# A two-layer decoder step with experts: the first chunk of layer 1's memory projection is computed inside pack 0 of layer 0's experts, and filling products take its place in layer 0's routing

## The reference, cut to what matters

```
for i in range(DEPTH):                       # both layers, before the trunk
    kv = rmsnorm(mem_prompt, mem_norm[i]) @ w_mem_kv[i]      # 256 x 1024 @ 1024 x 2048
    ...                                      # keys, values of layer i, also outputs
...
h = rmsnorm(x, norm_mix[i]);  z = h @ w_in
x = x + concatenate([mix, cross_attn(q, mem_k[i], mem_v[i])]) @ w_out
x = x + hier_moe(rmsnorm(x, norm_ffn[i]), ...)
```

## Time and profile before

| | us |
|---|---|
| median of the 3 timed executions | 1237.73 |
| lowest and highest | 1232.91, 1238.44 |
| the profiled execution | 1237.39 |
| its span, first to last instruction | 1235.6 |
| TensorE busy | 1170.5 (95%) |
| TensorE weight loads | 689.7 |
| VectorE busy | 356.5 |
| ScalarE busy | 154.2 |
| read from and written to HBM | 339.34 MB and 24.32 MB |

### The profile page before, as it was taken

How to read it: one execution, slowest core, us unless ns; L and a number is a source line. 1 busy time by engine, 2 the same in 40 slices (tenths; PEclk the granted TensorE clock), 3 DMA queues, 4 the chain that set the end, 5 groups by cost and what they waited for, 6 DMA issues and landing times.

```text
span 1235.6 us, 13751 instructions
## 1 busy us (share of the span) xinstructions
PE 1170.5 (95%) x5928; PEld 689.7 (56%) x5928; DVE 356.5 (29%) x870; ACT 154.2 (12%) x363; POOL 11.8 (1%) x22
## 2 busy tenths in 40 slices
PE   6999999999999998989999999999999999997886
PEld 5567776677554342436655656566667753432333
DVE  4222224112213141335224242424301022432225
ACT  2000002012111110110201011010200021110002
POOL 0000000000000000000000000000000000000000
PEclk9999999999999999999999999999999999999898
DMA  9953336833599999999234657392985469999994
GB/s 384 427 186 136 136 136 282 340 136 136 234 426 424 428 429 427 429 426 427 109 136 191 243 190 294 137 356 115 414 363 186 155 245 428 412 428 427 427 428 169
DMA packets 28159, 364.59 MB, mean 295 GB/s; under 512 B 3280, under 2 KB 3296, under 8 KB 5056
## 3 DMA queue, kind: packets, MB, share of 16 engines
q1 hardware_dynamic: 25200, 339.87, 67.2%
q10 hardware_dynamic: 1712, 19.17, 3.7%
q0 software_dynamic: 1184, 4.63, 1.0%
HBM read 339.34 MB, written 24.32 MB: 294 GB/s over the span
## 4 chain that ended last, share of the span: by engine, by line
PE 85%; DMA 12%; DVE 2%; issue 1%; ACT 1%; SPq 0%; DVEq 0%
PE bank L766 23%; PE bank L496 13%; DMA ring<-in_gu 11%; PE bank L604 7%; PE bank L582 5%; PE bank L401 5%; PE bank L849 5%; PE bank L406 4%; PE bank L636 4%; PE bank L614 3%; PE bank L820 1%; PE bank L452 1%; PE bank L930 1%; PE bank L419 1%; PE bank L475 1%; PE bank L911 1%
## 5 line engine op out<-in xcount | busy, mean ns | idle before, releaser
L766 PE MATMUL bank<-hT,ring 128*128 128x288 f32 x1088 | 268.2, 407 | 0.9 <-issue 0.9
L766 PEld LDWEIGHTS bank<-hT,ring 128*128 128x128 f32 x1088 | 205.7, 190 | 66.9 <-issue 12.0
L496 PE MATMUL bank<-arena,ring 128*128 128x288 f32 x640 | 158.5, 407 | 1.8 <-DVEq L1305 1.8
L496 PEld LDWEIGHTS bank<-arena,ring 128*128 128x128 f32 x640 | 120.2, 190 | 34.2 <-issue 2.2
L604 PE MATMUL bank<-ring,arena 128*32 128x512 f32 x944 | 115.3, 629 | 24.2 <-DMA ring<-in_gu 24.2
L582 PE MATMUL bank<-arena 128*128 128x512 f32 (+1 forms) x192 | 96.5, 628 | 0.2 <-DVE arena L1380 0.2
L604 PEld LDWEIGHTS bank<-ring,arena 128*32 128x32 f32 x944 | 30.4, 113 | 101.2 <-issue 82.5
L636 PE MATMUL bank<-arena 128*128 128x288 f32 x256 | 68.8, 413 | 2.8 <-issue 2.4
L401 PE MATMUL bank<-arena,ring 128*128 128x256 f32 x256 | 60.1, 398 | 9.4 <-DMA ring<-in_wkv 9.4
L582 PEld LDWEIGHTS bank<-arena 128*128 128x128 f32 (+1 forms) x192 | 31.5, 189 | 65.0 <-issue 63.9
L1397 DVE TENSOR_TENSOR xT<-xT,bank 128x288 f32<-128x288 f32 x128 | 58.2, 455 | 33.0 <-PE bank L636 29.2
(11 more groups left out here) (245 smaller groups left out, 846.4 us busy)
## 6 DMA issues: line engine op xcount, KB each, us to landing
ring<-in_gu SPq DMA_DIRECT2D x59, 2048.0 KB, 22.0
ring<-in_dn SPq DMA_DIRECT2D x32, 2048.0 KB, 19.8
ring<-in_rin SPq DMA_DIRECT2D x14, 2048.0 KB, 13.2
ring<-in_cin SPq DMA_DIRECT2D x8, 2048.0 KB, 24.5
ring<-in_kc SPq DMA_DIRECT2D x8, 2048.0 KB, 7.7
ring<-in_vc SPq DMA_DIRECT2D x8, 2048.0 KB, 10.5
ring<-in_st SPq DMA_DIRECT2D x8, 2048.0 KB, 10.4
out_rs<-ring ACTq DMA_DIRECT2D x8, 2048.0 KB, 8.4
```

The costliest lines, as they stand in the source:

```text
L496: mm = pe.matmul(bank[1 + o % 4][:, 0:T], w[:, k, :], cat[:, k, :], start=(k == 0), stop=(k == kt - 1))
L766: mm = pe.matmul(outs[o], w[:, o, k, :], src[:, k, :], start=(k == 0), stop=(k == KD - 1))
```

## The change

`MEMORY_IN` gets an entry for pack 0 (chunk 0), and chunk 0's weights leave the end of `SEQ_A`. So `pack_sequence(0)` puts them behind the four gate/up transfers of pack 0 and ahead of its down transfers: gate/up have now the places 24 to 27, chunk 0 the place 28, the down transfers 29 and 30 as before. Every later transfer keeps its place. `route(0)` has the filling products of `route(1)`. The two products of chunk 0 stand in pack 0 behind `pick(1)`, use PSUM banks 4 and 7 as those of the other chunks do (3 and 4 before), and are followed by the wait on ScalarE's copies. `memory_ahead(0)` is called from ScalarE's `experts` and no longer between its routing and the experts.

```
-SEQ_A = (... + [("vc0", c) for c in range(4)] + [("cout", c) for c in range(4)] + [("kv1", 0)])
-MEMORY_IN = {1: 1, 3: 2, 5: 3}
+SEQ_A = (... + [("vc0", c) for c in range(4)] + [("cout", c) for c in range(4)])
+MEMORY_IN = {0: 0, 1: 1, 3: 2, 5: 3}
...
-            KV_BANKS = ((0, 1, 2, 3, 4, 5, 6, 7), (3, 4, 4, 7, 4, 7, 4, 7))
+            KV_BANKS = ((0, 1, 2, 3, 4, 5, 6, 7), (4, 7, 4, 7, 4, 7, 4, 7))
...
             def route(i):
-                if i == 0:
-                    memory_kv(1, 0)
-                else:
-                    for _ in range(FILL):
-                        pe.matmul(bank[3][:, :], C("ident"), C("decay")[:, 0:512], start=True, stop=True)
+                for _ in range(FILL):
+                    pe.matmul(bank[3][:, :], C("ident"), C("decay")[:, 0:512], start=True, stop=True)
                 pe.wait_ge(S("htok_out"), KD * (i + 1))
                 pe.wait_ge(S("chosen"), i + 1)
...
-                if i == 0:
-                    memory_kv(1, 1)
-                else:
-                    pe.matmul(bank[3][:, :], C("ident"), C("decay")[:, 0:512], start=True, stop=True)
+                pe.matmul(bank[3][:, :], C("ident"), C("decay")[:, 0:512], start=True, stop=True)
...
-                    if L == 0 and i == 0:
-                        pe.wait_ge(S("kv1_out"), 2)
                     if L == 0 and i in MEMORY_IN:
                         j = 2 * MEMORY_IN[i]
                         memory_kv(1, j)
-                        pe.wait_ge(S("gt_out"), i)
+                        if i:
+                            pe.wait_ge(S("gt_out"), i)
                         memory_kv(1, j + 1)
                         pe.wait_ge(S("kv1_out"), j + 2)
...
             route(0)
-            memory_ahead(0)
             experts(0)
```

More of the change, by code:

```diff
@@ L55 @@
 SEQ_A = ([("kv0", c) for c in range(4)] + [("cin", c) for c in range(8)] + [("kc0", c) for c in range(4)]
-         + [("vc0", c) for c in range(4)] + [("cout", c) for c in range(4)] + [("kv1", 0)])
-MEMORY_IN = {1: 1, 3: 2, 5: 3}
+         + [("vc0", c) for c in range(4)] + [("cout", c) for c in range(4)])
+MEMORY_IN = {0: 0, 1: 1, 3: 2, 5: 3}
 def pack_sequence(l):
@@ L1032, in memory_ahead @@
                     dst = KT[:, 2 * j:2 * j + 2, :] if c < 2 else v3(V[:, j % 2, (c - 2) * 512:(c - 1) * 512], 2)
-                    act.activation(dst, v3(bank[(3, 4, 4, 7, 4, 7, 4, 7)[j]][:, :], 2), ACT.Copy) \
+                    act.activation(dst, v3(bank[(4, 7, 4, 7, 4, 7, 4, 7)[j]][:, :], 2), ACT.Copy) \
                        .then_inc(S("kv1_out"), 1)
```

## The result

Measured with 22 executions of each kernel, the changed one takes 1239.58 us (1237.24 to 1243.56) and the one before 1236.86 (1232.91 to 1239.12): a ratio of 1.0026, 95% interval 1.0018 to 1.0033. That is 2.2 to 4.1 us slower. The forecast was 3.0 us slower, 1240.7. It took 0.5% as the least that a measurement can tell; with 22 executions of each the interval is 0.15% wide, and 3 us are clear of no change. The profiled execution has a span of 1238.7 against 1235.6.

The account below looks back on a forecast made before the run. Layer 0's expert-weight transfers were taken as the bound. TensorE 10.8 us earlier, then 14.70 added: 3.9 late, less 0.9 in hand, gives 3.0 on the 1235.6 span; timed forecast 1240.7 us, range 1235.5 to 1244.0.

Parts of the forecast that it names:

- What bounds the stage: Layer 0's experts: weight transfers at 421 and 427 GB/s; landings set by the stretch's start and whether the queue runs dry.
- Part 1: Layer 0's routing: two products of 15.2 us removed, 14.50 us remain, first gate/up product 10.8 us earlier.
- Part 2: Chunk 0 in pack 0: 14.70 us added on TensorE, unhidden, so pack 1's gate/up products come 3.9 us later.
- Part 3: Ring order of transfers: costs nothing; pack 1's first gate/up issue at 319.4, 1.7 us earlier.
- The sum: Pack 2's down transfers: queue dry for 3.8 us, second landing 3.0 us late, kept to the end; 1240.7 us.
- dry a second time at 386.9: Pack 2's second down transfer, forecast issue 386.8, finds the queue empty again and lands 7.7 us later.
- the 0.9 us that the second down transfer had in hand: Pack 2: its landing took 8.6 us, 0.9 more than on an empty queue, so 3.9 late becomes 3.0.
- The earlier start: Rival: queue doesn't run dry at 377, all landings keep the 1.7 us, 1236.0; chance 0.10.
- The clock: Rival: two more 3.4 us half-clock stretches between 303 and 387 make landings 6.4 us late, 1244.1; chance 0.06.

Follow-up runs that it names:

- The ring order alone: Kernel before with only chunk 0's weights moved behind pack 0's gate/up weights, its products still in layer 0's routing: 1247.33 us, 1.0080.
- the filler run: Kernel before with five filling products of 512 columns added in pack 0 behind the wait for ScalarE's copies: 1238.32 us, 1.0015.
- the chunks apart: Changed kernel with the four memory chunks in packs 0, 2, 4 and 6 instead of 0, 1, 3 and 5: 1236.95 us, 0.9999.
- The run with packs 0, 2, 3 and 5: Changed kernel with memory chunk 1 moved from pack 1 to pack 2, stores as before: 1237.04 us, 1.0014.
- The late-store run: Changed kernel with the 1 MB store of layer 1's keys issued after layer 0's experts instead of at 378.9: 1238.69 us, 1.0015.
- the run with packs 1, 3, 5 and late stores: Kernel before, chunks left in place, with the stores of layer 1's keys and values issued after layer 0's experts: 1233.32 us, 0.9971.

## Why the prediction was right

**What bounds the stage** was right: the stream of transfers, its start and its dry places. The ring order alone (1.0080) shows the first; of the second the filler run shows the landings, and the chunks apart (0.9999) the time. The run with packs 0, 2, 3 and 5, where the hole is closed and the time is still 1.0014, is not explained.

**Part 1** was right to 0.1 us: 14.5 us for the routing, 10.8 saved. Why the rest stays was put down to ranking and selection with the fillers at no price of their own. The run without fillers shows that they pay: without them that routing would have been 4.2 us longer.

**Part 2** was right to 0.1: 14.70 added, TensorE 4.0 late instead of 3.9.

**Part 3** was right: first issue 319.4, second down transfer of pack 1 issued at 345.4 with the queue full, nothing lost.

**The sum** had the right mechanism, the dry place ahead of pack 2's down transfers, with its price too small. Two of its steps did not happen as written. The queue was not dry a second time at 386.9, because the store that it left out was running there. And the 0.9 us that the second down transfer had in hand were not given back: TensorE was 4.0 us later at that issue and the landing 4.3 us later, and in the filler run 4.3 and 4.3. (In the second profile of the kernel before, this landing took 8.9 us and not 8.6, so the 0.9 was not a firm number either.)

On an empty queue I let the second down transfer land 7.7 us after its issue; it took 8.9, and 9.0 in the second profile. The late-store run splits this. With the store gone the landing is 7.6, but the transfer behind comes 6.1 instead of 4.9 later, and the lateness from there is the same 4.2 us; the run with packs 1, 3, 5 and late stores, on a nearly empty queue, has 6.2. So an emptied queue costs some 1.2 us more than the landing of its first transfer tells; why, no run shows. With it the sum is 4.2 where I had 3.0; measured are 4.3 at that landing, 3.95 at the handoff (3.1 in the second pair of profiles). That the span says 3.1 and the ratio 3.2 is then partly luck. The 0.8 us between 3.95 and 3.1 also separate the two profiles of the kernel before, so they don't belong to the change.

**The rivals.** The earlier start did not win, since the queue did run dry; with the chunks apart it nearly did (0.9999). The clock took no part in the first profile of the changed kernel, which has full clock from 307.8 until 1010, through all of layer 0's experts; it was right to fear it where work is light, as the run without fillers shows. The rule of the Trainium skill ("TensorE: Matmul & The Clock Gate", HAM oscillation) that was weighed there agrees with that run: 13.6 us at 0.50 with TensorE waiting between short products, against 3.4 us with the fillers. By the Trainium skill, "DMA: Bandwidth & Descriptors", Anatomy of one DMA, the sum would have been 2.2 us; the landings say 4.2, which is further from it than from my 3.0, and the measurement decides.

## What to carry to other kernels

Where a stage is a stream of transfers, look for the issue that finds the queue nearly empty: that is where the computing engine's lateness turns into lateness of the stream. Its landing time against that on an empty queue (here 8.6 against 7.7) looked like lateness that could be given for nothing, but in both runs that were about 4 us late there the landing was late by all of it; whether less than 0.9 us would be free was not tried. A start gained ahead of a dry place was lost in it. In counting the stream, count the stores of other queues too. Before leaving work in or taking it out, see which bytes of the stream have no need to be there: taking two stores of 1 MB out of it gave 3.6 us, and 5.6 with one chunk moved a pack later, where moving the chunk into pack 0 had cost 3.2.

## What the runs showed of the hardware

- After a transfer that found the queue empty (issue to landing 7.6 us for 2 MB), the next 2 MB landed 6.1 us later, and after one that found it nearly empty (7.5 us) 6.2 us later, with 4.9 us per transfer on a full queue. Another that found it empty took 8.6 us.
- A store from ScalarE's queue into a hole of SyncE's stream cost nothing up to the landing at 400.6; in the full stream 1 MB cost 2.5 us (handoff 5.0 us earlier without two).
- The granted clock behind the same wait for weights at 537 was 1.00 in one execution and 0.50 for 6.8 us in another of the same program; the spans differ by 3.3 us, 2.8 of it behind that wait. So a single pair of profiles can't carry a verdict on 3 us.
- The half clock that began in layer 0's routing lasted 3.4 us under filling products and 13.6 us without them (TensorE busy 10.25 of 13.4 us), over `pick(0)`, which took 10.28 instead of 5.99 us.
